# Layer norms folded into per-chunk sums and finished off TensorE's path, in a transformer pair on one core

## What is computed

```python
h = h + gate[:, None] * mixed                  # end of the first block
return rmsnorm(h, final_g)                     # x * rsqrt(mean(x^2) + 1e-6) * final_g
...
h = layernorm(x, ln_in_g, ln_in_b)             # start of the second block, eps 1e-5
proj = h @ w_in                                # q, k, v, o, gates, conv parts
...
h = layernorm(ALPHA * h + mix, ln1_g, ln1_b)   # mix = concat(y_conv, y_m) @ w_out
ff = peer_ffn(h, peer_wq, keys, u, v)          # queries, top-16 keys, experts
h = layernorm(ALPHA * h + ff, ln2_g, ln2_b)    # the output
```

## Time and profile before

| | us |
|---|---|
| median of 3 runs | 3049.94 (3046.16 to 3050.68) |
| the profiled execution's own time | 3052.07 |
| its span, first to last instruction | 3050.4 |
| TensorE matmul busy | 2893.8 (95%) |
| VectorE busy | 1663.1 (55%) |
| ScalarE busy | 1338.5 (44%) |
| GpSimd busy | 620.3 (20%) |
| mean granted TensorE clock | 0.975 |

### The profile page before, as it was taken

How to read it: one execution, slowest core, us unless ns; L and a number is a source line. 1 busy time by engine, 2 the same in 40 slices (tenths; PEclk the granted TensorE clock), 3 DMA queues, 4 the chain that set the end, 5 groups by cost and what they waited for, 6 DMA issues and landing times.

```text
span 3050.4 us, 52640 instructions
## 1 busy us (share of the span) xinstructions
PE 2893.8 (95%) x16728; PEld 2537.8 (83%) x16728; DVE 1663.1 (55%) x3163; ACT 1338.5 (44%) x2517; POOL 620.3 (20%) x488
## 2 busy tenths in 40 slices
PE   7999999799989699999799999999999999999996
PEld 7987878788767698998699998888888888888885
DVE  2143245322455545676688775555555666666666
ACT  2132244222444345445344455555554555555553
POOL 1100001300000000000000287787752111111110
PEclk9999999899989799999899999999999999999998
DMA  7843355943435356456555677787777666666774
GB/s 264 283 134 95 97 153 172 334 134 97 124 115 174 99 159 191 154 161 206 165 166 178 173 180 188 188 192 188 188 200 254 216 217 217 217 217 217 216 213 130
DMA packets 183006, 554.36 MB, mean 182 GB/s; under 512 B 53776, under 2 KB 53808, under 8 KB 179600
## 3 DMA queue, kind: packets, MB, share of 16 engines
q1 hardware_dynamic: 136656, 500.25, 53.0%
q0 software_dynamic: 45696, 48.88, 6.8%
q10 hardware_dynamic: 576, 4.19, 0.4%
HBM read 532.13 MB, written 21.10 MB: 181 GB/s over the span
## 4 chain that ended last, share of the span: by engine, by line
PE 49%; DVE 1%; ACT 0%; issue 0%; ACTq 0%; DVEq 0%
PE PS L1727 11%; PE PS L162 11%; PE PS L163 11%; PE PS L164 11%; PE PS L1729 6%; PE PS L1698 0%; DVE stats L279 0%; DVE hb L2008 0%; PE PS L254 0%; DVE hb L289 0%; DVE hb L288 0%; DVE w_lo L153 0%; DVE wj_lo L1776 0%; DVE h L268 0%; ACT h L262 0%
## 5 line engine op out<-in xcount | busy, mean ns | idle before, releaser
L153 DVE TENSOR_TENSOR w_lo<-raw,w_hi 128x512 fp32r<-128x512 f32 x1696 | 1180.5, 718 | 911.9 <-ACT w_hi L146 907.9
L146 ACT ACTIVATE w_hi<-raw 128x512 fp32r<-128x512 f32 x1696 | 1029.6, 629 | 915.3 <-PE PS L164 823.7
L1727 PE MATMUL PS<-h,w_hi 128*128 128x512 f32 x1504 | 521.6, 391 | 2.0 <-DVE w_lo L153 2.0
L1640 POOL DMA_INDIRECT g_dram<-gt,spot x256 | 417.7, 1632 | 449.9 <-DVE gt L1968 340.0
L1729 PE MATMUL PS<-h,w_lo 128*128 128x256 f32 x1504 | 422.0, 281 | 0.0
L162 PE MATMUL PS<-w_hi,wj_hi 128*128 128x512 f32 x1024 | 399.6, 390 | 3.8 <-DVE wj_lo L1776 3.8
L163 PE MATMUL PS<-w_lo,wj_hi 128*128 128x512 f32 x1024 | 399.4, 390 | 0.0
L164 PE MATMUL PS<-w_hi,wj_lo 128*128 128x512 f32 x1024 | 399.3, 390 | 0.0
L1727 PEld LDWEIGHTS PS<-h,w_hi 128*128 128x128 f32 x1504 | 281.3, 187 | 63.4 <-DVE w_lo L153 2.4
L1729 PEld LDWEIGHTS PS<-h,w_lo 128*128 128x128 f32 x1504 | 285.1, 190 | 0.0
L162 PE MATMUL PS<-h,w_hi 128*128 128x256 f32 x800 | 229.9, 287 | 5.0 <-DVE w_lo L153 2.9
(11 more groups left out here) (326 smaller groups left out, 4362.6 us busy)
## 6 DMA issues: line engine op xcount, KB each, us to landing
raw<-in_u_s SPq DMA_DIRECT2D x256, 512.0 KB
raw<-in_v SPq DMA_DIRECT2D x256, 512.0 KB
raw<-in_w_in_s SPq DMA_DIRECT2D x112, 512.0 KB
raw<-in_w_mod_s SPq DMA_DIRECT2D x64, 512.0 KB
raw<-in_w_in_a SPq DMA_DIRECT2D x64, 512.0 KB
raw<-in_w_in_b SPq DMA_DIRECT2D x64, 512.0 KB
raw<-in_w_out_s SPq DMA_DIRECT2D x64, 512.0 KB
raw<-in_w_gate_s SPq DMA_DIRECT2D x32, 512.0 KB
```

Of the source, the lines that this page charges most:

```text
L146: act.activation(w_hi[m % 2][:, half], raw[:, m % NRAW, half], ACT.Copy).then_inc(hi_ready, 1)
L153: dve.tensor_tensor(w_lo[m % 2][:, half], raw[:, m % NRAW, half], w_hi[m % 2][:, half].bitcast(F), ALU.subtract).then_inc(lo_ready, 1)
L1640: pool.indirect_dma_start(g_dram, bass.IndirectOffsetOnAxis(spot[:, t, h, k:k + 1], 0), gt[:, t, h, k:k + 1], None, compute_op=ALU.add).th ...
L1727: pe.matmul(PS[:, 6 + j % 2, :], w_hi[m % 2][:, c], h_both[:, kk, :, :].rearrange("p a t -> p (a t)"), start=(kk == 0), stop=False)
```

## The change

- The root-mean-square norm and the layer norm behind it are taken as one. With w = x·`final_g`, the layer norm of x·r·`final_g` (r the inverse root of the mean square) is (w − mean(w)) / sqrt(var(w) + 1e-5·(mean(x²) + 1e-6)). Sums of x² (ScalarE) and statistics of w (VectorE) are taken by chunk, between the slabs of the next chunk.
- The statistics give a scaled tile z = (w − mean)·inverse deviation; z is transposed, and the norm's weight and bias are applied behind the transposes, where a feature is a partition (`affine_act`, `affine_dve`, with columns `lnc`). The new reader of the transposed rows takes four banks, and the first products begin while later transposes run (`first_products`). The token-major h, which is needed later, is made by GpSimd from z (`finish_h`), in two products and two sums of 128x2048. The same is done for the second norm (`zb`), and GpSimd stores h to `h_dram`.
- The last two slabs of both output projections are multiplied tile by tile (`last_pair`).
- The end: the last four v slabs are loaded in another order and multiplied chunk by chunk; residual and statistics follow each chunk; the two passes and the store go by parts of 1024, 512 and 512 columns.
- Output projection 1: transposes through four banks, the loop over chunks written out, residual work in four pieces between slabs, the table of ScalarE's Sqrt loaded before the slabs.

The core of the diff:

```diff
+        def first_products(pe, out, src, m, x_hi, x_lo, z_tr, from_act, from_dve, parted):
+            for b in range(5):
+                transpose_z(pe, src, b, z_tr, from_act, from_dve)
+            for b in range(KT // 2):
+                half, k0 = b // 4, 2 * b % 8
+                pe.wait_ge(parted, b + 1)
+                if k0 % 4 == 0:
+                    pe.wait_ge(lo_ready, 2 * (m + half) + (k0 // 4 + 1))
+                for k in (k0, k0 + 1):
...
+                if b < 3:
+                    transpose_z(pe, src, b + 5, z_tr, from_act, from_dve)
+        def affine_dve(dve, b, y, g, z_tr, parted, from_dve):
...
+                i = dve.tensor_scalar(y[:, b % 4, k, :], PS[:, BANKS[b % 4], k * T:(k + 1) * T],
+                                      lnc[:, g, kk:kk + 1], lnc[:, g + 1, kk:kk + 1], ALU.mult, ALU.add)
+        def head_dve(dve, y, g, x_hi, x_lo, m, z_tr, from_dve, head_hi, parted):
+            def lo(b):
+                dve.wait_ge(head_hi, b + 1)
+                dve.tensor_tensor(x_lo[:, 2 * b:2 * b + 2, :], y[:, b % 4, :, :], x_hi[:, 2 * b:2 * b + 2, :].bitcast(F),
+                                  ALU.subtract).then_inc(parted, 1)
+            affine_dve(dve, 1, y, g, z_tr, parted, from_dve)
+            split_slab(dve, None, m)
...
+            affine_dve(dve, 7, y, g, z_tr, parted, from_dve)
+            split_slab(dve, None, m + 1)
+            for b in range(4, KT // 2):
+                lo(b)
+        def last_pair(pe, outs, m, x_hi, x_lo, first_tile):
+            for t in range(TT):
+                tok = slice(t * P, (t + 1) * P)
+                for g in (6, 7):
...
+                if t == 0:
+                    last.then_inc(first_tile, 1)
+        def finish_h(pool, hz, z_tr, par, par_in, made):
+            pool.wait_ge(z_tr, KT // 2)
+            pool.wait_ge(par_in, 32)
+            for x, op in enumerate((ALU.mult, ALU.add)):
+                if x:
+                    pool.wait_ge(made, TT)
+                for t in range(TT):
+                    pool.tensor_tensor(hz[:, t, :], hz[:, t, :], par[x][:, :], op).then_inc(made, 1)
...
@@ output projection 1, VectorE @@
+                        for i in range(N_OUT - 1):
+                            split_slab(dve, None, m0 + i + 1)
+                            c = i // 8 - 1
+                            if c >= 0 and i % 8 == 1:
+                                wait_multiplied(dve, None, m0 + 8 * c + 8)
+                                gate(c, tiles)
+                                dve.sem_inc(gated, 1)
+                            if c >= 0 and i % 8 == 2:
+                                add(c, tiles)
+                            if c >= 0 and i % 8 == 3:
+                                weigh(c, tiles)
+                            if c >= 0 and i % 8 == 4:
+                                gather(c, tiles)
...
+                        dve.wait_ge(first_tile, 1)
+                        gate(3, [0])
+                        add(3, [0])
+                        weigh(3, [0])
+                        gather(3, [0])
+                        sums(0)
...
+                        scale_of(dve, step, 1).then_inc(scaled, 1)
+                        dve.wait_ge(scaled, 2)
+                        z_dve(dve, h_buf, 1, slice(0, D // 2))
@@ second block, GpSimd @@
+                for i, name in enumerate(("ln_in_g", "ln_in_b")):
+                    pool.dma_start(par[i][:, :], bcast(io[name])).then_inc(ln_in, 16)
                 pool.memset(z[:, :, 0:2], 0.0)
                 pool.memset(v2[:, :, :, P:P + 1], 1.0).then_inc(zeroed, 1)
+                finish_h(pool, h_buf, z_tr, par, ln_in, h_made)
@@ queries, GpSimd @@
+                    finish_h(pool, zb, z_tr, par_h, ln_in, h_made)
+                    pool.wait_ge(h_made, 2 * TT)
+                    pool.dma_start(h_dram, zb[:, :, :]).then_inc(h_stored, 16)
@@ the end, TensorE @@
-                    for n in range(N_KEYS - 2, N_KEYS):
-                        for a in range(2):
-                            expert_slab(None, v0 + 2 * n + a, n, a, False, n == N_KEYS - 1)
+                    for q in range(4):
+                        for n in range(N_KEYS - 2, N_KEYS):
...
+                            for t in range(TT):
+                                tok = slice(t * P, (t + 1) * P)
+                                last = mm3(pe, PS[:, 4 * t + q, :], (wj_hi[n % 2][:, tok], wj_lo[n % 2][:, tok]),
```

More of the change, by code:

```diff
@@ L242, in peer_block_kernel @@
             at += n
-        def transpose_in(pe, src, sem_src, copied, done, banks=(0, 1)):
-            for b in range(KT // 2):
[L248 to L269, removed]
+        BANKS = (0, 1, 2, 3)
@@ L274, in peer_block_kernel @@
         mv = keep("mv", [P, TT, 8])
[L276 to L289, removed]
+        lnc = keep("lnc", [P, 4, KT])
         with ExitStack() as first:
@@ new lines, in root @@
+                        def root(t):
+                            act.wait_ge(asked, t + 1)
+                            act.activation(mv[:, t, 3:4], mv[:, t, 2:3], ACT.Sqrt).then_inc(given, 1)
+                        act.preload_act_table(ACT.Sqrt)
+                        for i in range(N_OUT - 1):
+                            round_slab(act, None, m0 + i + 1)
+                            if i >= 8 and i % 8 == 4:
+                                for t in range(TT):
+                                    square(i // 8 - 1, t, 2 * (i // 8 - 1))
@@ L1030, in _ @@
[L1030 to L1037 removed]
+                        dve.wait_ge(xin, 48)
+                        dve.wait_ge(padded, 1)
@@ L1356, in _ @@
                 step = chain(dve, "dve_in2")
-                transposed_split(dve, h_hi, h_lo, rnd, cp, banks=(6, 7))
+                head_dve(dve, y_in, 0, h_hi, h_lo, m0, z_tr, from_dve, head_hi, parted)
+                for s in range(1, NRAW):
+                    split_slab(dve, None, m0 + s + 1)
                 dve.wait_ge(wg_round, 1)
@@ new lines, in _ @@
+                    for t in range(TT):
+                        for x, cols in enumerate(OUT_PARTS):
+                            if t == 0 and x == 0:
+                                step(dve.scalar_tensor_tensor(hb[:, t, cols], hb[:, t, cols], mv[:, t, 0:1], par[0][:, cols],
+                                                              ALU.subtract, ALU.mult))
+                                dve.wait_ge(given, TT)
+                                step(dve.reciprocal(mv[:, :, 4], mv[:, :, 3]))
+                            else:
+                                step(dve.scalar_tensor_tensor(hb[:, t, cols], hb[:, t, cols], mv[:, t, 0:1], par[0][:, cols],
+                                                              ALU.subtract, ALU.mult))
+                            dve.scalar_tensor_tensor(hb[:, t, cols], hb[:, t, cols], mv[:, t, 4:5], par[1][:, cols],
+                                                     ALU.mult, ALU.add).then_inc(ready, 1)
```

429 lines of the change are left out of this document (291 added, 138 removed).

## The result

Over 10 runs each, the changed kernel takes 3041.24 us (median, 3035.36 to 3051.03) and the kernel before 3056.84 us (3046.16 to 3064.86). The ratio is 0.9946, with a 95% interval of 0.9929 to 0.9962: faster by 0.54%, or 16.5 us (the medians themselves are 15.6 apart). The forecast was 10.3 us faster. The profiled execution of the changed kernel took 3042.07 us, its span is 3040.2.

A forecast was written before the change was run, and what follows sets the result against it. TensorE, with matmuls in 95% of the span, was taken as the bound, only its pauses and slow stretches winnable. Terms −2.5 −3.4 −18.6 −9.1 −7.4 +36.0 −5.3 gave −10.3 us, on the median 3039.6; range 3024 to 3053.

The forecast's parts named there:

- Item 1: Start of output projection 1: with four banks TensorE need not wait between transposes; −2.5 us.
- Item 6: Heads: GpSimd's four long operations take turns with VectorE's splits and hold up TensorE; +18.0 us each.
- Item 5: The two heads, without GpSimd: products begin after about five transposed banks, TensorE nearly always busy from then; −3.7 us each.
- Item 3: End of output projection 1: 8.1 us from last matmul to next stage in place of 26.7; −18.6 us.
- item 4: End of output projection 2: next stage starts after 4.7 to 5.2 us in place of 14.2; −9.1 us.
- Item 2: Body of output projection 1: TensorE's three waits for a split go, VectorE's operations being spread behind splits; −3.4 us.
- Item 7: The end: 20.7 us after the last matmul in place of 26.0; −5.3 us.
- A: Rival, heads: GpSimd does not hold up TensorE, 0 to 5 us each; about 3008 us, chance 0.12.
- B: Rival, heads: GpSimd's operations run through without giving VectorE a turn, 23.7 us or more each; 3051 to 3058, chance 0.12.
- C: Rival: the hold is as forecast, but the tails give less; 3044 to 3050 us, chance 0.16.

The follow-up runs named there:

- e5: The changed kernel with the last two slabs of both output projections multiplied for both tiles in turn; last matmul to next transpose 10.10 and 6.53 us.
- e6: The changed kernel with output projection 1's weight products and statistics of the first three chunks moved behind the last slabs; last matmul to next transpose 15.91 us.
- e7: The changed kernel with a chunk's four operations in one go behind the second slab of the next chunk; body of output projection 1 92.08 us.
- e3: The changed kernel with each 128x2048 GpSimd operation of the heads cut into eight pieces of 128x256; median 3019.77 us, ratio to before 0.9879.
- e4: The changed kernel with the heads' GpSimd operations in 128x512 pieces, these and the attention bias sums each waiting for a split; median 3013.57 us, ratio to before 0.9868.
- e1: The changed kernel without the four GpSimd products and sums of 128x2048 in each head; median 3013.01 us, ratio to before 0.9876.
- e12: The changed kernel run again unaltered, with a second trace; median 3032.57 us, ratio to before 0.9937.
- e2: The changed kernel with each 128x2048 GpSimd operation of the heads cut into four pieces of 128x512; median 3018.38 us, ratio to before 0.9893.
- e8: The changed kernel with the end's residual additions and statistics behind the last split, passes and stores in whole rows; last matmul to span's end 20.89 us.
- e11: The kernel of e4 with the output gate's 128x2048 GpSimd product in four of 128x512, each behind a split; median 3000.59 us, ratio to before 0.9823.

## Why the prediction was right, and where it was not

The time lies in the range, and the sign and the mechanism are as forecast. That the sum came so close is luck: the parts that the change touches gave 13.0 us more than forecast (items 1 and 6 5.1 and 9.6 more, item 5 3.6 less), and in the profiled execution the parts before them took 13.1 back.

- **Item 3 and item 4, the tails:** 8.06 and 4.97 us against 8.1 and 4.7 to 5.2. Adding up single operations from their rows along two engines was exact. e5 and e6 show both of its ingredients, +2.0 and +7.9 when undone.
- **Item 2, the body:** −3.5 against −3.4, and e7 brings the waits back.
- **Item 1, the start:** −7.6 against −2.5. The failed step is "end after 6.5, plus ... 1.4: about 7.9": transposes to first gate operation took 6.1 us (889.60 to 895.68). What was left out is the clock. In this execution the transposes were 0.11 us apart, the full level; in e3 the same code had them 0.21 apart, the lower level, and this step took 8.0 us, just the forecast. The gate matmuls too ran at the full clock, and the first product came 6.55 us behind the first of them, in place of 8.5; in e4 the same code stayed at 1.2 GHz there (8.8 us), and its start took 17.9 us. Over the traces of the new code this term is −3.6 to −7.6.

Rows of the first product, in the changed kernel and in e4 (0.47 and 0.77 us for the same matmul, and 0.23 or 0.43 from one to the next behind it):

```profile
902.56 0.47 PE L162 MATMUL PS<-w_hi,oc_hi 128*128 128x512 f32 x1
902.87 0.39 PE L163 MATMUL PS<-w_lo,oc_hi 128*128 128x512 f32 x1
903.10 0.40 PE L164 MATMUL PS<-w_hi,oc_lo 128*128 128x512 f32 x1
```
```profile
894.50 0.77 PE L162 MATMUL PS<-w_hi,oc_hi 128*128 128x512 f32 x1
...
895.07 0.63 PE L163 MATMUL PS<-w_lo,oc_hi 128*128 128x512 f32 x1
895.50 0.63 PE L164 MATMUL PS<-w_hi,oc_lo 128*128 128x512 f32 x1
```

- **Item 5, the heads without GpSimd:** −2.5 and −1.3 against −3.7 each. The first product came at 5.15 us, as said. The step that failed is "TensorE is nearly always busy from then on": after 24 products it waited 2.2 us in e1 for a low part of VectorE, restarted at the lower level, and had its 48 products done at 16.9 and 16.7 us, not 14.6. In e12 it came out of the same wait at the full level and was done at 15.25. Rows of that wait in the second head, in the changed kernel and in e12 (the next matmuls 0.21 us apart in one, 0.12 in the other):

```profile
1482.39 0.58 PE L162 MATMUL PS<-h,w_hi 128*128 128x256 f32 x1 [2.13 <-DVE h L322]
```
```profile
1471.24 0.39 PE L162 MATMUL PS<-h,w_hi 128*128 128x256 f32 x1 [2.12 <-DVE h L322]
```

- **Item 6, GpSimd's operations:** the mechanism holds: 20.95 us against 20.6, a split in each turn, and the cost is gone without the four operations (e1) and a third as large in pieces (e2). That 20.95 is so near is in part luck, since 1.5 of it is GpSimd's own wait. Its size was 14.0 and 12.4 against 18. The step that failed is "in 20.6 us TensorE gets 5.7 us of work": it got 76 matmuls, 9.1 us. Two more splits were through before GpSimd's first operation could work, which itself waited (6.09 us in place of 4.54). In the first head the broadcasts had landed late, 14.8 us into the stage and not at 11 to 13. In the second they landed at 12.6, as forecast, and there VectorE kept its turn for one more low part and two splits. "By then the head is nearly split, so little comes off" was the term sized too low. The forecast clock "near 0.5" was 0.84: behind two of the four pauses the matmuls came at the full level. Where GpSimd came sooner (e7) the cost was 18.4.
- **Item 7, the end:** −6.9 against −5.3. The last store took 2.5 us where 3.3 was taken, and the sums 5.0 where 5.6. e8 divides it: 4.3 come from the order of the products, 1.8 from early sums and parts, and 0.9 from a store whose time differed without a known cause.
- **What no item had:** 13.1 us in parts that nothing changed, of which 8.8 are one run-through of the bias sums. A forecast against a single profiled execution carries such a term unseen.
- **Rivals.** A (no hold) is out by e1. B's mechanism exists, but not in the heads. C is out, as the tails gave what they should. In B's sum item 2 is taken with 2.4 us unused where its own bounds leave 3.4, so 3058 should read 3059; nothing hangs on it.

The Trainium skill (SBUF — State Buffer, on the shared port pair and its lock) says that the engine that comes second is blocked for the whole of the other's operation. The trace agrees: splits of 5.02 us beside operations of 4.5, and 0.69 without. It says that the loser waits, but not whose turn is next, and that made the difference between 1.2 and 10.9 us at 569 us.

## What to carry to other kernels

Count what a helper engine holds, not what it does. Four GpSimd operations of 4.5 us beside a VectorE that feeds TensorE cost 12 to 18 us here, though GpSimd is busy in only 22% of the span; the same work in pieces of 128x512, each behind a semaphore that the fed engine passes anyway, cost nothing here: with that the gain over the kernel before was 41 us (e4) and, with the last long operation cut as well, 56 (e11), in place of 16 to 24.

Work that can be summed by chunk belongs between slabs, one operation at a time: in one go behind a chunk it cost 6.1 us, spread out nothing (e7).

Lay two traces over each other by instruction number before comparing totals. A difference of 10 us in the end was 23 gained and 13 lost elsewhere.

## What the runs showed of the hardware that was not expected

- The order of turns at the shared port is not fixed. The sixteen sums of 128x256 took turns with splits in nine traces (a waiting split 1.2 us) and ran through in two (10.7 and 10.9 us). In the changed kernel's trace the split's record even starts first, 569.36 against 569.40. VectorE can run through as well: at 1483 us it finished a low part and did another and two splits, 0.69 us each, while GpSimd's operation waited 2.2 us. Between two long operations (128x2048) one VectorE operation came through every time, in every trace that has them.
- Which level of the clock follows a pause cannot be told from the length of the pause alone. In the first head of the changed kernel matmuls were 0.12 us apart behind pauses of 2.0 us and 0.21 apart, the lower level, behind 3.0 and 3.25. But in the second head the lower level followed a pause of 2.13 (1482.39) and the full level one of 3.24 (1495.36, for four matmuls, then the lower), and in e12 a pause of 2.02 was followed by the lower level (1024.23).
- Matmuls of the u stage can take 9.9 us longer in an execution (677.5 against 667.6), evenly over the loop, at clock 1.00. Its cause stays open.
